# Output projections of a two-block fp32 layer: values stationary and 512 weight columns moving, instead of weights stationary and 256 token columns moving

## The reference

```python
h = rms_norm(x, norm1_g);  u = h @ w_in          # 13 parts: attention, state space, gates
# ... three mixers y_a, y_b, y_c ...
mix = g0 * (y_a @ w_br_dsa) + g1 * (y_b @ w_br_nsa) + g2 * (y_c @ w_br_ssd)
x = x + mix @ w_out                               # w_out  1024 x 1024
h = rms_norm(x, norm2_g)
x = x + square(relu(h @ w_ff1)) @ w_ff2           # w_ff2  4096 x 1024
# even mixer: ya from a 31-tap convolution and a layernorm, yb from pooled differences
x = x + concat([ya, yb]) @ w_out_even             # 2048 x 1024: rows of ya, rows of yb
# odd mixer: ly from a gated linear recurrence of width 1536
x = x + ly @ w_out_odd                            # 1536 x 1024
return rmsnorm(x, final_norm)
```

## Time and profile before

| | us |
|---|---|
| runs of the kernel | 1085.14 median of 1084.55, 1085.14 and 1087.7 |
| the profiled execution, its span | 1085.7 |
| PE busy | 1042.7, 96% |
| DVE, ACT, POOL busy | 695.8, 610.4, 588.5 |
| moved by DMA | 158.08 MB, 146 GB/s in the mean |

### The profile page before, as it was taken

One profiled execution on the slowest core, in us unless ns is written; L12 is line 12 of the kernel. 1 busy time (PEld: TensorE's weight loads), 2 busy tenths in 40 slices (PEclk: granted clock), 3 DMA queues, 4 the chain that ended last, 5 costly groups with the idle time before them and its releaser, 6 DMA issues.

```text
span 1085.7 us, 21365 instructions
## 1 busy us (share of the span) xinstructions
PE 1042.7 (96%) x8145; PEld 979.9 (90%) x8145; DVE 695.8 (64%) x1467; ACT 610.4 (56%) x1237; POOL 588.5 (54%) x448
## 2 busy tenths in 40 slices
PE   8999999999999999999999999999999998899896
PEld 8799988988889898989999999999899988889896
DVE  7869576666664425685485553332799976788864
ACT  5454557666665447764455655444434446568953
POOL 3656345454454459645534344346768875467652
PEclk9999899999999999999999999999999999999999
DMA  8234333333234442324555555555444543634442
GB/s 311 96 120 151 100 115 108 107 117 117 99 102 131 139 138 96 98 98 155 182 168 175 178 190 177 187 182 175 158 166 162 175 151 123 212 124 149 148 163 78
DMA packets 43157, 158.08 MB, mean 146 GB/s; under 512 B 4912, under 2 KB 4912, under 8 KB 42672
## 3 DMA queue, kind: packets, MB, share of 16 engines
q1 hardware_dynamic: 42912, 156.69, 43.5%
q10 hardware_dynamic: 144, 0.03, 0.0%
HBM read 155.65 MB, written 1.05 MB: 144 GB/s over the span
## 4 chain that ended last, share of the span: by engine, by line
PE 73%; DVE 14%; ACT 6%; issue 3%; POOL 2%; DMA 1%; DVEq 0%; ACTq 0%; SPq 0%; POOLq 0%
PE p_proj L1835 20%; PE p_proj L1836 19%; PE p_proj L1837 19%; PE p_score L1673 4%; PE p_proj L1820 3%; PE p_pv L1701 2%; DVE ring_lo L579 2%; ACT ring_hi L914 2%; DVE arena_r L1178 2%; PE p_turn L1683 1%; POOL ring_lo L579 1%; DVE arena L1399 1%; PE p_score L1593 1%; PE p_score L1741 1%; DVE arena_r L587 1%
## 5 line engine op out<-in xcount | busy, mean ns | idle before, releaser
L1835 PE MATMUL p_proj<-arena_r,ring_hi 128*128 128x256 f32 x2208 | 654.9, 297 | 18.8 <-POOL ring_lo L579 10.5
L1836 PE MATMUL p_proj<-arena_r,ring_hi 128*128 128x256 f32 x2208 | 626.7, 284 | 0.0
L1837 PE MATMUL p_proj<-arena_r,ring_lo 128*128 128x256 f32 x2208 | 626.3, 284 | 0.0
L579 POOL TENSOR_TENSOR ring_lo<-ring,ring_hi 128x1024 fp32r<-128x1024 f32 x178 | 427.9, 2407 | 291.7 <-ACT ring_hi L914 290.8
L1835 PEld LDWEIGHTS p_proj<-arena_r,ring_hi 128*128 128x128 f32 x2208 | 424.9, 192 | 38.1 <-issue 21.4
L1836 PEld LDWEIGHTS p_proj<-arena_r,ring_hi 128*128 128x128 f32 x2208 | 425.4, 193 | 7.4 <-issue 6.0
L1837 PEld LDWEIGHTS p_proj<-arena_r,ring_lo 128*128 128x128 f32 x2208 | 425.1, 193 | 0.0
L914 ACT ACTIVATE ring_hi<-ring 128x1024 fp32r<-128x1024 f32 x276 | 290.3, 1052 | 94.4 <-PE p_proj L1837 91.4
L579 DVE TENSOR_TENSOR ring_lo<-ring,ring_hi 128x1024 fp32r<-128x1024 f32 x98 | 125.1, 1276 | 71.9 <-ACT ring_hi L914 70.4
L688 POOL TENSOR_TENSOR sbuf_s<-sbuf_s,srow 128x256 f32<-128x256 f32 (+1 forms) x48 | 41.7, 870 | 83.1 <-DVE srow L1381 58.2
L937 ACT ACTIVATE arena_r<-arena 128x256 fp32r<-128x256 f32 x108 | 42.4, 409 | 39.8 <-DVE arena L1552 22.3
(11 more groups left out here) (287 smaller groups left out, 1163.9 us busy)
## 6 DMA issues: line engine op xcount, KB each, us to landing
ring<-w_stream SPq DMA_DIRECT2D x286, 512.0 KB, 3.3
arena<-w_tok SPq DMA_DIRECT2D x1, 1632.0 KB, 12.8
arena<-w_rgi SPq DMA_DIRECT2D x1, 1536.0 KB, 6.4
arena<-x_t SPq DMA_DIRECT2D x4, 256.0 KB, 6.5
arena<-w_cmp SPq DMA_DIRECT2D x1, 1024.0 KB, 15.7
out_t<-arena SPq DMA_DIRECT2D x4, 256.0 KB, 2.6
par<-cols SPq DMA_DIRECT2D x1, 323.0 KB, 3.3
row<-rows ACTq DMA_DIRECT2D x1, 32.0 KB, 3.5
```

The costliest lines, as they stand in the source:

```text
L579: return eng.tensor_tensor(ring_lo[:, u % RING, :, :].rearrange("p k n -> p (k n)"), ring[:, u % RING, :, :].rearrange("p k n -> p (k n)") ...
L1835: pe.matmul(slot(s)[:, 0:S], w_hi, hi, start=(c == 0), stop=False)
L1836: pe.matmul(slot(s)[:, 0:S], w_hi, lo, start=False, stop=False)
L1837: mm = pe.matmul(slot(s)[:, 0:S], w_lo, hi, start=False, stop=(c == n - 1))
```

## The change

Five products change sides: `w_out`, `ff2`, the two halves of the even output (`even_yb`, `even_ya`) and `odd_out`. Now 128 tokens of one input chunk are the block that is loaded, and 512 weight columns stream. One result is 128 tokens x 512 output channels and fills a PSUM bank; a product has four of them (channel half `fh`, token block `t`). A unit of the stream holds 2 input chunks x 512 columns, and a step `("tm", name, fh, u, t)` is six matmuls; each unit is used by two such steps. The last two units of a half are taken as u, u+1 for the first token block and then u, u+1 for the second.

`x` is now kept token by token in `sbuf_s` (loaded by a DMA of its own, `x_tok`, issued on SP before a unit of `br_ssd`). DVE adds the four results to it (`res`). A row holds all channels of a token, so the sum of squares is taken along it by ACT's Square with an accumulator (`sq`, four per norm) in place of `nsq`, `nacc` and `nsum`. For the next stage PE turns `x` back (`xt`, 16 transposes of 128x128 for each of the three borders) into PSUM, from where ACT and DVE make the hi and lo parts, and for the even and odd mixers ACT copies the turned `x` into `A(XT + c)` (`xcopy`). For these two, two columns of reciprocals are spread over the partitions by a matmul with a diagonal matrix (`bcast`) and a copy by ACT (`spread`). In `ff1` nothing is scaled by the norm any more: DVE multiplies the results of `ff2` by 1 over the mean square instead.

The first two jobs after a border (three after `ff2` and `even_ya`) are cut in two halves of four chunks (`half`), and their second halves come after the turned second half of `x`. The final norm is done for each token block on its own.

```diff
+    def residual(q, tag=None, follow=()):
+        name, n = CLOSES[q], TOKENS[CLOSES[q]]
+        for half in range(2):
+            for u, t in token_parts(name):
+                out.append(("tm", name, half, u, t))
+                if half == 1 and u == 0 and tag:
+                    out.append(("xt", q, 0, t))
+                    if t == 1:
+                        for c in range(4):
+                            out.extend([("split", tag, c), ("lo", tag, c)])
+                        if q > 1:
+                            out.extend([("xcopy", q, 0), ("xcopy", q, 1)])
+                if half == 1 and (u, t) == (n - 2, 1) and tag:
+                    out.append(("xt", q, 1, 0))
+                if u == n - 1:
+                    out.extend([("res", name, half, t)])
...
+        a, b = follow[0], follow[1]
+        out.extend([("half", a, 0), ("xt", q, 1, 1), ("half", b, 0), ("half", a, 1), ("half", b, 1)])
+        for c in range(4, 8):
+            out.extend([("split", tag, c), ("lo", tag, c)])
+        out.append(("sq", q, 1, 1))
+        if q > 1:
+            out.extend([("xcopy", q, 2), ("xcopy", q, 3), ("stat", q)])
+            out.extend([("half", follow[2], 0), ("bcast", q), ("half", follow[2], 1)])
...
+                elif k == "tm":
+                    _, name, fh, u, t = s
...
+                    if t == 0:
+                        pe.wait_ge(sem("w_lo_pool" if on_gpsimd(unit) else "w_lo_dve"), lo_turn[unit])
+                    for m in range(2):
...
+                        pe.matmul(slot(key), hi, w_hi, start=(c == 0), stop=False)
+                        pe.matmul(slot(key), lo, w_hi, start=False, stop=False)
+                        mm = pe.matmul(slot(key), hi, w_lo, start=False, stop=(c == n - 1))
...
+                    elif tag in TURNED:
+                        if c < 4:
+                            act.wait_ge(sem("xt_done"), TURNED[tag])
+                        else:
+                            take(("xT", TURNED[tag], 2 + c % 2))
+                        if c % 4 >= 2:
+                            act.wait_ge(sem(f"lo_{tag}"), c - 1)
```

More of the change, by code:

```diff
@@ L48 @@
           ("dq", 8, 8), ("nq", 8, 8), ("xbc", 24, 8), ("sz", 16, 8), ("mg", 24, 8),
[L49 to L53, removed]
+          ("br_dsa", 8, 8), ("br_nsa", 8, 8), ("br_ssd", 8, 16),
+          ("ff1", 32, 8), ("val_glu", 16, 8), ("b_val", 8, 8), ("b_gate", 8, 8),
+          ("a_gate", 8, 8), ("pool", 8, 2), ("xr", 12, 8), ("gate", 12, 8)]
+ON_VECTOR = {"br_dsa", "br_nsa", "br_ssd", "ff1", "xr"}
+TOKENS = {"w_out": 4, "ff2": 16, "even_yb": 4, "even_ya": 4, "odd_out": 6}
+TOKEN_TAG = {"w_out": "mix", "ff2": "ff", "even_yb": "yb", "even_ya": "ya", "odd_out": "ly"}
+CLOSES = {1: "w_out", 2: "ff2", 3: "even_ya", 4: "odd_out"}
+HALVED = [("job", "ff1", 0), ("job", "ff1", 1)] + [("job", "val_glu", j) for j in range(3)] \
+    + [("job", "xr", j) for j in range(3)]
 ON_POOL = {"ly": 9, "ya": 6}
@@ L100, in schedule, with token_parts @@
     jobs = {name: [("job", name, i) for i in range(n)] for name, n, _ in PHASES}
[L102 to L118, removed]
+    def token_parts(name):
+        n = TOKENS[name]
+        return [(u, t) for u in range(n - 2) for t in range(NT)] + [(n - 2, 0), (n - 1, 0), (n - 2, 1), (n - 1, 1)]
@@ L208, in schedule @@
         out += [("mgr", c), jobs["br_ssd"][c], ("split", "mix", c)]
-    squared(1, jobs["w_out"], "h1")
+    residual(1, "h1", jobs["ff1"])
     for j in range(34):
         if j < 32:
[L212 to L215, removed]
+            out += [jobs["ff1"][j], ("ffr", j)]
         if 1 <= j < 33:
@@ L235, in schedule @@
         out.append(job)
-        if job == val_glu[0]:
-            out += [("nsum", 2, 0), ("nsum", 2, 6), ("nsum", 2, 7), ("norm", 2)]
+        if job == val_glu[1]:
+            out.append(("spread", 2))
         if len(LATE_EVEN) > done:
@@ L305, in schedule @@
     out += [("scanout", 10), ("scanout", 11)] + [("split", "ly", c) for c in range(9, 12)]
[L306 to L317, removed]
+    residual(4)
+    splits = {}
+    starts = opening(out)
+    for u, s in enumerate(starts):
+        if s[1] not in PLAIN:
+            splits.setdefault(("units", u) if u < AHEAD else starts[u - AHEAD], []).append(("wsplit", u))
     final = []
@@ L556, in program @@
         hi_turn = {u: n + 1 for n, u in enumerate(split_units)}
[L557 to L560, removed]
+        unit_of = {u: s[1] for u, s in enumerate(opening(steps))}
         def on_gpsimd(u):
@@ L1803, in _ @@
                     fresh = tag not in seen
-                    if name not in PLAIN:
+                    if name not in PLAIN and span != 0:
                         seen.add(tag)
```

345 lines of the change are left out of this document (257 added, 88 removed).

## The result

The changed kernel takes 1090.66 us, the median of 18 runs (1087.53 to 1094.76), against 1086.78 for the kernel before (18 runs, 1083.7 to 1087.99): 1.0038 times as long, interval 1.0026 to 1.005. It is slower by 0.4%, where 1082 was forecast; the rival "spacing" had said 1089. The profiled execution has a span of 1086.9 us, 1.2 more than that of before, and lies low among its own runs (1088.58 beside a median of 1090.66). A run's time is longer than the span of its core by 1.7 to 1.8 us wherever both are listed, so the span of 1085.7 before stands for a time of some 1087.5; that it lay "0.6 us above the median" compared a span with times.

A forecast was written before the change was run, and what follows sets the result against it. PE, busy 96% of the span, was taken as the bound. Stage terms -1.3 + 0.3 + 3.1 - 6.8 = -4.7 us, with 1.5 for a clock fall -3.2, took 1085.7 to 1082.5, so 1082; range 1068 to 1094.

The forecast's parts named there:

- spacing: Rival for the streamed steps: 13.3 ns beyond the columns stay with every matmul, 7.2 us more, 1089 us; chance 0.25.
- the 1.5 for the clock: Added to the summed stages: one more fall of PE's clock after a wait, turning -4.7 into -3.2 us.
- I take 215.8 ns: Steady part of the five products: a 512-column matmul's time, making a step of six 1.295 us against 1.44.
- price of 0.65 us a ns: Kernel time per ns added to each 512-column matmul; above about 226 ns the kernel is slower by over 0.3%.
- a floor: Matmuls at 1.2 GHz: no excess shows, read as fitting a fixed time that a longer stream covers.
- The borders: Between stages: PE waits for POOL remainders behind ACT's block; after ff2, third job at 10.4 us, reciprocals at 12.8.
- `even`: Even output and its border: 75.09 us before, a loss of 3.1 forecast from longer waits and a longer chain.
- 1.3 earlier: End of even_ya, at 949.4: start 2.2 earlier, one POOL wait grown to 3.3, a second of 4.5.
- The tail: After odd_out: 7.7 us, 4.4 for residual, Square, root and scaling, 3.3 for the store with the end.
- Borders cheaper: Rival at stage borders: half-jobs and transposes fill PE's waits, a gain of about 24 us, 1061 in full; chance 0.18.
- halfway 1071: Borders, within the rival of cheaper borders: time in us if half of its full gain comes.
- Borders dearer: Rival at stage borders: DVE's lo takes 2.10 rather than 0.48, or clock falls at each; 1085 to 1092; chance 0.10.

The follow-up runs named there:

- the run with both moves: Changed kernel with hi parts of the half's last weight unit and the third job's unit moved ahead of ACT's x hi parts: 1074.33 us, 0.9879 of the kernel before.
- the run with the wait in the middle moved: Changed kernel with the hi part of the second half's last weight unit ahead of ACT's x block (w_out, ff2, even_ya): 1081.44 us, 0.9949 of the kernel before.

## Why the prediction was wrong

| us, without the 1.5 for the clock | before | forecast | forecast with 226.7 ns | after |
|---|---|---|---|---|
| w_out and border | 32.87 | 31.6 | 32.5 | 31.84 |
| ff2 and border | 111.99 | 112.3 | 116.3 | 116.61 |
| even and border | 75.09 | 78.2 | 78.9 | 77.14 |
| odd_out and tail | 46.74 | 40.0 | 41.6 | 42.05 |
| sum | 266.69 | 262.1 | 269.3 | 267.64 |

- **The step that failed** is "I take 215.8 ns". It drew on the plain float32 rows, as the only ones with as many cycles, and on the missing excess at 1.2 GHz in the earlier trace rows. The rows of the same kind of matmul, fp32r with 256 columns, had 13.3 ns beyond their columns everywhere at 2.4 GHz, and that is what 512 columns have. The rival had it right, and its 1089 is within 2 us of the median. That it is so near is partly luck: its four sums come to 1.7 us more than was measured, and the median of before came out 1.6 us higher in 18 runs than in the three that the forecast started from. Its price of 0.65 us a ns was a little high, 0.57.
- **At 1.2 GHz** 512 columns show no excess either: behind the wait at 912.78 in the run with both moves, at a granted clock of 0.50, starts are 0.43 apart, and 512/1.2 is 0.427.

```profile
913.93 0.63 PE L1779 MATMUL p_proj<-ring_hi,arena_r 128*128 128x512 f32 x1
914.35 0.63 PE L1780 MATMUL p_proj<-ring_hi,arena_r 128*128 128x512 f32 x1
914.78 0.63 PE L1781 MATMUL p_proj<-ring_lo,arena_r 128*128 128x512 f32 x1
```

  So that it is missing there does not mean that a longer stream covers it at 2.4 GHz. I had read a floor into it.
- **By the Trainium skill** ("TensorE: Matmul & The Clock Gate", section "Back-to-back issue gap") the isolated gap of a matmul of 512 columns is 512/2.4 + 2.5 ns, 216. The runs show 227 in a stream with a block loaded for each, and the measurement decides. Its other figure for 512 in a stream, 131 ns, no run here came near.
- **The borders** were right in kind and place: waits for POOL's remainder in the middle of a half and ahead of the third job, because ACT does a block of work for x first; forecast 2.2, 2.2 and 4.5 us in the middle, measured 1.88, 1.75 and 3.58; the third job of `val_glu` 9.4 us after the last step (10.4 forecast), the reciprocals at 13.2 (12.8), `b_val` 13.15 behind them (13.1), and 13.15 again with both moves (767.93 less 754.78). That the moves of ACT's order alone take them away shows it.
- **`even`** came out near its forecast (61.23 us to the last step, for 61.65), but by luck. The terms that are given don't make "1.3 earlier": 32 steps save 4.6, and the grown wait and the second one cost 1.0 and 4.5, so 0.9 later, even without the transposes. And the 2.31 of the earlier trace rows did not grow to 3.3: near that place PE now waits 1.76 us for DVE's residual and 0.51 for a remainder (ahead of 924.84 and 927.01).
- **The tail** was right: 7.94 us for 7.7.
- **The clock** was about right in size, as far as the runs tell. One fall at 1.5 us was added. This profile has falls at both border waits of 2.86 us (0.94 and 0.89 in their stretches), where before the borders were at 1.00, and none in `even_ya`, where before there was one. How many there are differs from run to run: the runs of the changed kernel under 1088.7 us have a mean granted clock of 0.991 to 0.994, those over 1093 one of 0.985 to 0.987. A straight line through its 18 runs gives 0.67 us for each 0.001 of that clock. The 26 runs of before that stand beside the experiments have 0.993 in the mean, these 18 have 0.990: by that, an estimate, some 2 of the 3.9 us go with the clock. No run fixes the number of falls.
- **What a fall costs** depends on what PE waits for next. The same wait for POOL at the last unit of `even_yb` has no fall behind it in the changed kernel (first two rows) and one in the run with the wait in the middle moved (last two, 0.50 from 917 to 920):

```profile
918.70 0.50 PE L1767 MATMUL p_proj<-ring_hi,arena_r 128*128 128x512 f32 x1 [2.30 <-POOL ring_lo L645]
924.84 0.50 PE L1767 MATMUL p_proj<-ring_hi,arena_r 128*128 128x512 f32 x1 [1.76 <-DVE sbuf_s L1253]
...
916.38 0.55 PE L1777 MATMUL p_proj<-ring_hi,arena_r 128*128 128x512 f32 x1 [2.31 <-POOL ring_lo L655]
922.52 0.50 PE L1777 MATMUL p_proj<-ring_hi,arena_r 128*128 128x512 f32 x1 [0.18 <-DVE sbuf_s L1263]
```

  From the one start to the other it is 6.14 us both times: the fall only took up the wait for DVE.
- **"Borders cheaper"** was held against with ACT's order, rightly for this order; with those weight units moved the same steps reach 1074 and 1072, near its halfway 1071.
- **"Borders dearer"** named two things. DVE's `lo` did not take 2.10: all 24 that read PSUM took 0.48. Falls of the clock did come at two borders.

## What to carry to other kernels

Take the start-to-start time of a matmul from rows of the same type and the same pattern of loads, not from rows of another type that happen to last as long: take an excess per instruction to stay with each instruction until a run shows otherwise; then its halved count is all that a longer stream gains. When work for the next stage is put between two stages, look where on the casting engine the next weights stand: a unit or two at each border, moved ahead of such a block, turned a change that lost 0.4% into one that gained 1.2%.

## What the runs showed that was not expected

In a steady stream an fp32r matmul with a newly loaded block takes its columns at 2.4 GHz plus 13.3 ns at 256 and at 512 columns, but takes 111 ns at 128, where 53 are columns. At 1.2 GHz neither 256 nor 512 columns have anything on top, as far as the rows can tell (213 and 427 ns). What the 13.3 ns are, and whether the block's load sets the pace at 128, is not shown: every matmul of these runs has a load of its own. And a wait of 2.86 us cost 4.1 us at one border, as the clock fell behind it, and 3.2 at another, while a fall at the end of `even_yb` cost nothing: PE had to wait for DVE behind it anyway.
